# Token halves for the last three tiles of two down projections in a one-core encoder layer

## The chip, the cores and the metric

One core of a Trainium2 chip runs the whole program. Its engines are TensorE (PE in the views; PEld is its weight load), VectorE (DVE), ScalarE (ACT), GpSimd (POOL) and SyncE (SP), which issues most DMAs. The metric is the device time in microseconds, the median of several runs.

## What is computed

The reference, cut to the layer (DEPTH is 1, 512 tokens of width 1024, 16 meta tokens in front, so 528 rows until the last of them are dropped):

```python
h = layer_norm(concatenate([meta, x]), ln_in_g, ln_in_b)
h = layer_norm(ALPHA * h + 0.5 * swiglu(h, gate1, up1, down1), ffn1_ln_g, ffn1_ln_b)
h = layer_norm(ALPHA * h + token_mixer(h, ...), mix_ln_g, mix_ln_b)
h = layer_norm(ALPHA * h + 0.5 * swiglu(h, gate2, up2, down2), ffn2_ln_g, ffn2_ln_b)
return h[:, 16:]
# swiglu: (silu(h @ gate) * (h @ up)) @ down, inner width 2816
# token_mixer: h @ w_in, then windowed attention and a two-way gated linear attention, then @ w_out
```

## The kernel before

Activations lie transposed: eight tiles of 128 features (KD = 8), each with all tokens in its free dimension. Every float32 product is made of three fp16 products: weights and activations are split into a high and a low half, and `PRODUCTS` lists the three pairs.

**Weights.** A chunk of weights is loaded into one of two buffers of `stage`. VectorE takes the largest value of each partition (`chunk_max`, L1413), GpSimd takes the largest over the partitions, VectorE works out a power of two in four small operations (`chunk_scale`, L1395 to L1400), ScalarE writes the high half (`split_hi`, L1059) into one of two buffers of `wsp`, and VectorE the low half (`chunk_lo`, L1435), which raises `w_ready`. Each engine's order is written out by hand. SyncE loads chunk c once chunk c - 2 is split.

**Down projection of either feed-forward block (`ffn`, f = 0 or 1).** Eight tiles q = 0 to 7 of the output, each of 22 slices of the inner width. The last three slices have a scale of their own and sum into other banks, so VectorE adds a tile in two steps, A (L1471, against `H`) and B (L1459, against `X`), and then adds the tile into `x_sum` (L1356). In the first block a tile is 132 matmuls of 264 columns, in the second 66 of 512. Chunks 0 and 1 of the down weights are split before the projection starts. In step q VectorE prepares the chunk of tile q + 1 (for q of 1 to 6) and then adds tile q. TensorE may start tile q when its weights are ready and tile q - 2 has been added.

**Norm (`layer_norm(L)`).** L = 1 and 3 follow the two feed-forward blocks, L = 2 the mixer. For each of two token halves: TensorE makes the mean by a matmul with a matrix of ones (`sum_tiles`, L499, and the last tile, L504), VectorE subtracts it (`centre`, L1363), ScalarE squares (L992), TensorE sums the squares (L510), ScalarE takes the root (L1042), VectorE the reciprocal (L1382). Then, tile by tile over all tokens, VectorE multiplies (L1386), ScalarE writes the fp16 input `xs` of the next matmuls and `H` (L1051, L1053), VectorE the low half of `xs` (L1376). After L = 3 SyncE writes `H` out.

**Start of the mixer.** `w_in` is used in 20 tiles: z (0), gk (1, 2), gq (3, 4), gv (5 to 16) and others. TensorE runs tiles 0 and 1 as the norm delivers `xs` (L632), then the others (L648), with small gate matmuls (L695) between. ScalarE empties each tile (`proj_out`, L1121), and a tile may start when the tile two before it is out. `gates_abs` (L1151) and `gates_ln` (L1158, L1160) are the start of the gate arithmetic on ScalarE; `gates` on VectorE carries it on.

Of the kernel before, what the change touches and what calls it, by code (L numbers as in the profile page):

```python
# [102 lines left out]
def build(nc, x_in, meta_in, params, rel_in, head_in, ident_in, masks_in, reset_in, w2_in,  # L103
          gate, up, down, w_in, w_out, out):
    with ExitStack() as ctx:
# [279 lines left out]
        GK, GQ, GV, GG, AQ, AK, AV = 1, 3, 5, 5 + 2 * NCH, 9 + 2 * NCH, 13 + 2 * NCH, 14 + 2 * NCH  # L385
        LAST_OF = [max(n for n, t in enumerate(TILES) if t[2] == c) for c in range(N_IN)]
# [32 lines left out]
        def ln_bank(L, square, h):  # L419
            return 4 * square + (h if L < 2 else 2 * h + 1)  # L420
# [30 lines left out]
        def _(sp):  # L451
# [15 lines left out]
            for f in range(2):  # L467
# [8 lines left out]
                with sp.Fori(0, N_DN // 2) as i:  # L476
                    for t in range(2):
                        sp.wait_ge(w_ready, DN[f] - 1 + t + 2 * i)
                        load_halves(down[f][2 * i + t], (DN[f] + t) % 2, DN_COLS)
# [14 lines left out]
        def _(pe):  # L494
            def sum_tiles(L):

                pe.wait_ge(x_summed, sums_before(L) + N_SUM)
                for h in range(2):
                    nc.tensor.matmul(PS[:, ln_bank(L, 0, h), 0:ln_width(L)], ones[:, :], x_sum[:, token_half(L, h)], start=True, stop=False)  # L499

            def layer_norm(L):
                for h in range(2):
                    pe.wait_ge(*((res_half, L) if h == 0 else (res_done, 2 + KD * L)))
                    nc.tensor.matmul(PS[:, ln_bank(L, 0, h), 0:ln_width(L)], ones[:, :], X[:, KD - 1, token_half(L, h)],  # L504
                                     start=False, stop=True).then_inc(mean_ready, 1)
                for h in range(2):
                    for k in range(KD):
                        n = ln_step(L, h, k)
                        pe.wait_ge(squared, n + 1)
                        nc.tensor.matmul(PS[:, ln_bank(L, 1, h), 0:ln_width(L)], ones[:, :], squares[:, n % 4, 0:ln_width(L)],  # L510
                                         start=k == 0, stop=k == KD - 1).then_inc(sq_added, 1)
# [62 lines left out]
            def res_tile(late, r, s, w, src, kt, k_sem=None, k0=0, norm=None, split_at=None, before_b=None):  # L574


                pe.wait_ge(res_done, r + 1)
                for k in range(kt):
                    if norm is not None and k == kt - 3:
                        sum_tiles(norm)  # L580
                    if k == split_at:
                        mm.then_inc(res_ready, 1)
                        if before_b is not None:
                            pe.wait_ge(*before_b)
                    if k_sem is not None:

                        pe.wait_ge(k_sem, k0 + k + 1)
                    b = split_at is not None and k >= split_at
# [1520 lines left out]
```

## Time and profile before

| | |
|---|---|
| Time, median of 3 runs | 1091.84 us (1091.57 to 1091.97) |
| Time of the profiled execution | 1082.67 us |
| Its span, first to last instruction | 1080.9 us |
| TensorE busy | 997.0 us (92%) |
| VectorE busy | 720.4 us (67%) |
| ScalarE busy | 382.2 us (35%) |
| Mean granted TensorE clock | 0.978 |

The span is the time between the first and the last instruction in the trace; the rest of the execution's time lies around it. Times below are microseconds from the span's start. A busy share is a mean over the whole span and says nothing of a single stage.

### The profile page before, as it was taken

What the parts mean: (1) busy time and instruction counts of PE and PEld (TensorE: products, weight loads), DVE (VectorE), ACT (ScalarE), POOL (GpSimd) and SP (SyncE); (2) the same over time, 40 slices, a digit from 0 to 9 for tenths busy, and PEclk for the clock granted to TensorE, in tenths of its full rate; (3) what the DMA queues carried; (4) which work ended last, traced back from release to release, by engine and by line L of the source; (5) the groups of instructions that cost most, each with busy time, mean ns of one, the idle gap of its engine ahead of it and who ended that gap; (6) DMA issues with size and microseconds to landing.
All of it is one profiled execution on the core that took longest, in us unless ns stands there. A gap on an engine that the chain in (4) does not pass through costs nothing.

```text
span 1080.9 us, 16392 instructions
## 1 busy us (share of the span) xinstructions
PE 997.0 (92%) x6605; PEld 654.4 (61%) x6605; DVE 720.4 (67%) x1186; ACT 382.2 (35%) x488; POOL 32.3 (3%) x96
## 2 busy tenths in 40 slices
PE   3999999999899988999996889699999999989995
PEld 2888888888688875985564434434444444434443
DVE  6766666668755667767659757666666667966645
ACT  5422222224411126754334741462222223531105
POOL 0000000000000000000000000000000000000000
PEclk9999999999899998999998999889999999999998
DMA  5323232323232121111211003112323223322202
GB/s 203 107 79 109 85 110 84 109 86 110 105 108 85 68 78 32 62 64 42 77 40 40 1 1 117 40 73 83 116 78 116 96 98 127 111 78 86 104 1 79
DMA packets 23808, 88.76 MB, mean 82 GB/s; under 512 B 2907, under 2 KB 3251, under 8 KB 23763
## 3 DMA queue, kind: packets, MB, share of 16 engines
q1 hardware_dynamic: 22752, 87.17, 22.7%
q10 hardware_dynamic: 1011, 0.99, 0.3%
q8 instruction: 29, 0.48, 0.2%
q14 instruction: 16, 0.13, 0.0%
HBM read 86.05 MB, written 2.10 MB: 82 GB/s over the span
## 4 chain that ended last, share of the span: by engine, by line
PE 75%; DVE 16%; ACT 6%; issue 2%; DMA 0%; ACTq 0%; POOL 0%; DVEq 0%
PE PS L553 35%; PE PS L593 20%; PE PS L648 8%; DVE cmax L1413 3%; DVE wsp L1435 3%; PE PS L944 3%; ACT wsp L1059 2%; PE PS L510 2%; PE PS L632 1%; DVE big L1513 1%; ACT H L1053 1%; PE PS L770 1%; DVE X L1363 1%; PE PS L922 1%; PE PS L766 1%
## 5 line engine op out<-in xcount | busy, mean ns | idle before, releaser
L553 PE MATMUL PS<-xs,wsp 128*128 128x264 f16 (+1 forms) x3168 | 472.7, 312 | 7.5 <-ACT xs L1051 4.0
L553 PEld LDWEIGHTS PS<-xs,wsp 128*128 128x128 f16 x3168 | 311.0, 98 | 168.4 <-issue 9.6
L1059 ACT ACTIVATE wsp<-stage,wscale 128x2048 f16<-128x2048 f32 (+2 forms) x73 | 156.5, 2144 | 369.9 <-DVE wscale L1399 198.0
L1435 DVE SCALAR_TENSOR_TENSOR wsp<-stage,wscale,wsp 128x2048 f16<-128x2048 f32 (+2 forms) x73 | 184.6, 2529 | 114.3 <-ACT wsp L1059 114.3
L593 PE MATMUL PS<-big,wsp 128*128 128x264 f16 (+1 forms) x1584 | 238.6, 314 | 11.6 <-DVE big L1513 9.5
L593 PEld LDWEIGHTS PS<-big,wsp 128*128 128x128 f16 x1584 | 155.8, 99 | 94.1 <-DVE big L1513 12.8
L1413 DVE TENSOR_REDUCE cmax<-stage 128x1 f32<-128x2048 f32 (+2 forms) x73 | 179.7, 2462 | 3.9
L1447 DVE SCALAR_TENSOR_TENSOR big<-PS,oscale,tmp_a 128x528 f32 (+3 forms) x44 | 33.4, 759 | 75.7 <-ACT tmp_a L1066 75.6
L1066 ACT ACTIVATE tmp_a<-PS,oscale 128x528 f32<-128x528 f32 (+1 forms) x44 | 30.5, 694 | 136.1 <-PE PS L553 136.1
L648 PE MATMUL PS<-xs,wsp 128*128 128x264 f16 (+1 forms) x384 | 67.0, 328 | 0.1
L2007 POOL PARTITION_ALL_REDUCE call<-cmax x73 | 27.9, 382 | 979.1 <-DVE cmax L1413 979.1
L648 PEld LDWEIGHTS PS<-xs,wsp 128*128 128x128 f16 x384 | 35.8, 98 | 24.4 <-issue 1.9
L944 PE MATMUL PS<-xs,wsp 128*128 128x512 f16 x192 | 42.3, 379 | 2.3 <-DVE X L1459 2.1
L648 PE MATMUL PS<-wsp,xs 128*88 128x256 f16 (+2 forms) x408 | 39.5, 257 | 1.7 <-ACT kT L1121 1.7
L1089 ACT ACTIVATE big<-big,hscale 128x528 f16<-128x528 f32 (+1 forms) x44 | 30.3, 722 | 29.1 <-DVE big L1513 26.6
L648 PEld LDWEIGHTS PS<-wsp,xs 128*88 128x88 f16 (+2 forms) x408 | 38.0, 113 | 3.5 <-ACT kT L1121 2.5
L1513 DVE SCALAR_TENSOR_TENSOR big<-big,hscale 128x528 f16<-128x528 f32 (+1 forms) x44 | 31.6, 755 | 5.0 <-ACT big L1089 3.8
L992 ACT ACTIVATE tmp_b<-X 128x256 f32<-128x256 f32 (+1 forms) x48 | 17.8, 416 | 46.6 <-DVE X L1363 45.3
L944 PEld LDWEIGHTS PS<-xs,wsp 128*128 128x128 f16 x192 | 18.5, 98 | 25.7 <-DVE wsp L1435 2.6
L510 PE MATMUL PS<-tmp_b,ones 128*128 128x256 f32 (+1 forms) x96 | 24.9, 417 | 9.9 <-ACT tmp_b L992 9.9
L1471 DVE SCALAR_TENSOR_TENSOR X<-PS,oscale,H 128x528 f32<-128x528 f32 (+1 forms) x16 | 12.2, 759 | 27.5 <-PE PS L593 27.4
L1403 DVE TENSOR_REDUCE hmax<-big (+2 forms) x44 | 30.1, 684 | 0.0
(208 smaller groups left out, 685.1 us busy)
## 6 DMA issues: line engine op xcount, KB each, us to landing
stage<-in_gate SPq DMA_DIRECT2D x44, 512.0 KB, 3.4
stage<-in_up SPq DMA_DIRECT2D x44, 512.0 KB, 4.2
stage<-in_down SPq DMA_DIRECT2D x32, 704.0 KB, 4.9
stage<-in_w_in SPq DMA_DIRECT2D x16, 512.0 KB, 4.4
stage<-in_w_out SPq DMA_DIRECT2D x8, 512.0 KB, 4.4
X<-in_x SPq DMA_DIRECT2D x4, 512.0 KB, 6.2
out_T<-H SPq DMA_DIRECT2D x8, 256.0 KB, 2.0
stage<-in_w_in SPq DMA_DIRECT2D x2, 576.0 KB, 4.4
```

The source lines that it names most:

```text
L510: nc.tensor.matmul(PS[:, ln_bank(L, 1, h), 0:ln_width(L)], ones[:, :], squares[:, n % 4, 0:ln_width(L)], start=k == 0, stop=k == KD - 1).t ...
L553: return nc.tensor.matmul(dst, w, x, start=k == 0 and wp + xp == 0, stop=k == KD - 1 and xp == 1)
L593: mm = nc.tensor.matmul(dst, w(wp, k), x, start=k in (0, split_at) and wp + xp == 0, stop=k + 1 in (kt, split_at) and xp == 1)
L648: mm = nc.tensor.matmul(dst, x if lhs_is_x else w, w if lhs_is_x else x, start=k == 0 and wp + xp == 0, stop=k == KD - 1 and xp == 1)
L944: mm = nc.tensor.matmul(acc(1, 2 * (n % 2)), w, tokens(1, xs[:, xp, k, :]), start=gla and k == REP and wp + xp == 0, stop=not gla and k == ...
L1059: nc.scalar.activation(wsp[:, slot, 0, 0:cols], stage[:, slot, 0:cols], ACT.Copy, scale=wscale[:, slot:slot + 1]).then_inc(w_hi, 1)
L1066: nc.scalar.activation(tokens(f, tmp_a[:, s, :]), acc(f, 4 * s), ACT.Silu, scale=oscale[:, slot:slot + 1]).then_inc(silu_ready, 1)
L1089: nc.scalar.activation(hid_s[:, m, 0, ln_cols(2 * f)], hid[:, m + 2, ln_cols(2 * f)], ACT.Copy, scale=hscale[:, i:i + 1]).then_inc(hs_hi, 1)
L1413: nc.vector.tensor_reduce(cmax[:, one], stage[:, slot, 0:cols], AX.X, ALU.max, apply_absolute_value=True).then_inc(w_max, 1)
L1435: nc.vector.scalar_tensor_tensor(wsp[:, slot, 1, 0:cols], stage[:, slot, 0:cols], wscale[:, one], wsp[:, slot, 0, 0:cols], ALU.mult, ALU.s ...
L1447: nc.vector.scalar_tensor_tensor(tokens(f, hid[:, m + 2, :]), acc(f, 4 * s + 2), oscale[:, slot:slot + 1], tokens(f, tmp_a[:, s, :]), ALU. ...
L1513: nc.vector.scalar_tensor_tensor(hid_s[:, m, 1, t], hid[:, m + 2, t], hscale[:, i:i + 1], hid_s[:, m, 0, t], ALU.mult, ALU.subtract).then_ ...
```

## The change

Tiles 0 to 4 of each down projection stay whole. Tiles 5, 6 and 7 are computed first for the first token half and then for the second, and the norm of the first half is done between and beside the matmuls of the second. So the weights of the three tiles must live longer: they get three buffers in `arena` (`w_extra`). The chunks are loaded and split in the order of `DN_ORDER`, and `DN_STEPS` says which of them VectorE prepares ahead of adding each whole tile. In the first block the projections z, gk and the first gq run by token halves too, and `gates(1)` stands two tiles later. A tiny square root (`warm`) stands ahead of each norm on ScalarE. In norm 2 the low half of the first gate/up chunk, the next chunk's maximum and its scale change places. The output is written in 16 halves instead of 8 tiles. No arithmetic is left out.

```diff
+N_FULL = 5
+DN_ORDER = [0, 1, 5, 2, 3, 6, 4, 7]
+DN_AT = [DN_ORDER.index(q) for q in range(N_DN)]
+DN_STEPS = [[2], [3], [4, 5], [6], [7]]
...
+        def w_down(f, q, part):
+            return wsp[:, (DN[f] + q) % 2, part, :] if q < N_FULL else w_extra[:, q - N_FULL, part, :]
...
 TensorE, ffn(f):
+                for q in range(N_FULL):
+                    down_tile(f, q)
+                down_tile(f, 5, 0)
+                down_tile(f, 6, 0)
+                down_tile(f, 7, 0, (KF - 3, lambda: sum_tiles(L, 0)))
+                down_tile(f, 5, 1, (8, lambda: mean(L, 0)))
+                square_sums(L, 0)
+                down_tile(f, 6, 1)
+                down_tile(f, 7, 1, (KF - 3, lambda: sum_tiles(L, 1)))
...
 TensorE, mixer_projections() (mean(1, 1) stands inside first_proj_tiles(0)):
-                first_proj_tiles()
-                proj_tile(GK + 1)
+                first_proj_tiles(0)
+                early_proj_tile(GK + 1, 0)
+                square_sums(1, 1)
+                early_proj_tile(GQ, 0)
+                first_proj_tiles(1)
+                early_proj_tile(GK + 1, 1)
                 gates(0)
+                early_proj_tile(GQ, 1)
+                proj_tile(GQ + 1)
                 gates(1)
-                for n in range(GQ, GV + NCH + 1):
+                for n in range(GV, GV + NCH + 1):
...
 TensorE, at the end:
-            layer_norm(3)
+            mean(3, 1)
+            square_sums(3, 1)
...
 ScalarE, ffn(f):
+                for n in itertools.chain(*DN_STEPS):
+                    q = DN_ORDER[n]
+                    c = DN[f] + n
+                    if q < N_FULL:
+                        act.wait_ge(res_ready_b, N_RES * f + q - 1)
+                    act.wait_ge(w_scale, 4 * c + 3)
+                    nc.scalar.activation(w_down(f, q, 0), stage[:, c % 2, 0:DN_COLS], ACT.Copy,
+                                         scale=wscale[:, c % 2:c % 2 + 1]).then_inc(w_hi, 1)
...
 VectorE, ffn(f):
+                for n in range(2):
+                    down_scales(n)
+                for q in range(N_FULL):
+                    for n in DN_STEPS[q]:
+                        down_chunk(n)
+                    down_residual(f, q)
+                for n, q in enumerate(range(N_FULL, N_DN)):
+                    if f == 0 and n < 2:
+                        c = IN0 + n
+                        chunk_max(c, c % 2, c // 2, KD * IN_COLS[n])
+                        split(c, c % 2, KD * IN_COLS[n], (XF_IN, XF_INQ)[n])
+                    down_residual(f, q, 0)
+                L = 2 * f + 1
+                centre(L, 0)
+                down_residual(f, 5, 1)
+                half_rstd(L, 0)
+                half_norm(L, 0, 0, 4)
+                down_residual(f, 6, 1)
+                half_norm(L, 0, 4, KD)
+                down_residual(f, 7, 1)
+                centre(L, 1)
+                half_rstd(L, 1)
+                half_norm(L, 1, 0, KD)
```

`down_chunk(n)` is `chunk_max`, `chunk_scale`, two small scales and the low half of one chunk; `down_residual` is the old A and B with the addition into `x_sum`; `half_norm` is the tile by tile part of the norm for one token half.

**VectorE at the start of the first down projection.** The rows of before begin behind the last low half of the hidden values (A, L1471, and B, L1459, add a tile; L1356 sums; L1413 starts a chunk, here that of tile 2, and L1435 ends it):

```order
L1471 SCALAR_TENSOR_TENSOR X<-PS,oscale,H 128x528
L1459 SCALAR_TENSOR_TENSOR X<-PS,oscale_b,X 128x528
L1441 TENSOR_TENSOR oscale<-winv,xinv 128x1
L1565 TENSOR_TENSOR oscale_b<-winv,xinv 128x1
L1413 TENSOR_REDUCE cmax<-stage 128x1
L1395 TENSOR_SCALAR cexp<-call 128x1
L1397 TENSOR_SCALAR cneg<-cexp 128x1
L1399 TENSOR_SCALAR wscale<-cneg 128x1
L1400 TENSOR_SCALAR winv<-cneg 128x1
L1435 SCALAR_TENSOR_TENSOR wsp<-stage,wscale,wsp 128x2816
```

The rows of the change begin behind the scales of chunks 0 and 1 (L1516 starts a chunk, L1693 ends it; L1569 and L1573 are A and B):

```order
L1516 TENSOR_REDUCE cmax<-stage 128x1
L1498 TENSOR_SCALAR cexp<-call 128x1
L1500 TENSOR_SCALAR cneg<-cexp 128x1
L1502 TENSOR_SCALAR wscale<-cneg 128x1
L1503 TENSOR_SCALAR winv<-cneg 128x1
L1682 TENSOR_TENSOR dscale<-winv,xinv 128x1
L1684 TENSOR_TENSOR dscale_b<-winv,xinv 128x1
L1693 SCALAR_TENSOR_TENSOR arena<-stage,wscale,arena 128x2816
L1569 SCALAR_TENSOR_TENSOR X<-PS,dscale,H 128x528
L1573 SCALAR_TENSOR_TENSOR X<-PS,dscale_b,X 128x528
L1516 TENSOR_REDUCE cmax<-stage 128x1
```

A whole chunk, that of tile 5, which goes to `arena`, now stands ahead of adding tile 0 and of tile 2's chunk.

**ScalarE at the start of the mixer.** Before, from the emptying of z, gk and gk (L1121) on (L1151 is `gates_abs`, L1059 a high half, the table loads belong to `gates_ln`):

```order
L1121 ACTIVATE big<-PS,oscale 32x528
L1121 ACTIVATE X<-PS,oscale 128x528 x2
L1151 ACTIVATE tmp_a<-PS,par 128x528 x2
L1059 ACTIVATE wsp<-stage,wscale 128x2048
L1158 ACT_TABLE_LOAD
L1158 ACTIVATE tmp_a<-tmp_a 128x1056
L1160 ACT_TABLE_LOAD
L1160 ACTIVATE tmp_a<-tmp_a 128x1056
L1121 ACTIVATE X<-PS,oscale 128x528 x2
L1059 ACTIVATE wsp<-stage,wscale 128x2048
L1121 ACTIVATE big<-PS,oscale 88x256
```

With the change (L1194 empties, L1224 is `gates_abs`, L1122 a high half):

```order
L1194 ACTIVATE big<-PS,oscale 32x528
L1194 ACTIVATE X<-PS,oscale 128x528 x3
L1224 ACTIVATE tmp_a<-PS,par 128x528
L1122 ACTIVATE wsp<-stage,wscale 128x2048
L1194 ACTIVATE X<-PS,oscale 128x528
L1224 ACTIVATE tmp_a<-PS,par 128x528
L1231 ACT_TABLE_LOAD
L1231 ACTIVATE tmp_a<-tmp_a 128x1056
L1233 ACT_TABLE_LOAD
L1233 ACTIVATE tmp_a<-tmp_a 128x1056
L1122 ACTIVATE wsp<-stage,wscale 128x2048
L1194 ACTIVATE big<-PS,oscale 88x256
```

The second `gates_abs` moved behind the emptying of both gq tiles, and the table loads with it; the first gv tile (88x256) is still emptied behind the high half that follows them.

**VectorE at norm 2.** Before, behind the sum of tile 6 (L1464 adds tile 7, L1435 and L1413 are the first and second gate/up chunk, L1363 centres, L1382 is the reciprocal):

```order
L1464 SCALAR_TENSOR_TENSOR X<-PS,oscale,H 128x256 x2
L1435 SCALAR_TENSOR_TENSOR wsp<-stage,wscale,wsp 128x2048
L1413 TENSOR_REDUCE cmax<-stage 128x1
L1363 TENSOR_TENSOR X<-X,PS 128x256 x16
L1395 TENSOR_SCALAR cexp<-call 128x1
```

With the change, from the same place (L1538 is the low half, L1592 adds tile 7, L1434 centres, L1516 is the maximum, L1484 the reciprocal):

```order
L1538 SCALAR_TENSOR_TENSOR wsp<-stage,wscale,wsp 128x2048
L1592 SCALAR_TENSOR_TENSOR X<-PS,oscale,H 128x256 x2
L1434 TENSOR_TENSOR X<-X,PS 128x256 x16
L1516 TENSOR_REDUCE cmax<-stage 128x1
L1484 RECIPROCAL stats<-stats 128x256 x2
L1498 TENSOR_SCALAR cexp<-call 128x1
```

The low half moved ahead of adding the last tile, the maximum behind the centring, and the small scale operations behind the reciprocals.

## Rows read from the trace of the kernel before

**Rows 1.** The page, the chain that ended last, by engine

```profile
PE 75%; DVE 16%; ACT 6%; issue 2%; DMA 0%; ACTq 0%; POOL 0%; DVEq 0%
```

**Rows 2.** Timeline of TensorE, norm 1: start, us, line, count, idle before

```profile
396.75 1.16 PE L504 MATMUL PS<-X,ones 128*128 128x264 f32 x4 [0.65 <-DVE X L1464]
...
412.79 1.04 PE L632 MATMUL PS<-xs,wsp 128*32 128x264 f16 x4 [4.10 <-ACT xs L1051]
...
428.59 5.56 PE L648 MATMUL PS<-xs,wsp 128*128 128x264 f16 x48
```

**Rows 3.** Timeline of VectorE, first down projection

```profile
289.21 0.15 DVE L1441 TENSOR_TENSOR oscale<-winv,xinv 128x1 f32<-128x1 f32 x1
...
292.18 3.08 DVE L1413 TENSOR_REDUCE cmax<-stage 128x1 f32<-128x2816 f32 x1
...
299.03 3.15 DVE L1435 SCALAR_TENSOR_TENSOR wsp<-stage,wscale,wsp 128x2816 f16<-128x2816 f32 x1 [2.71 <-ACT wsp L1059]
...
306.21 0.77 DVE L1459 SCALAR_TENSOR_TENSOR X<-PS,oscale_b,X 128x528 f32<-128x528 f32 x1 [1.23 <-PE PS L593]
...
335.91 0.77 DVE L1459 SCALAR_TENSOR_TENSOR X<-PS,oscale_b,X 128x528 f32<-128x528 f32 x1 [1.23 <-PE PS L593]
336.71 0.71 DVE L1356 TENSOR_TENSOR stats<-stats,X 128x528 f32<-128x528 f32 x1
```

**Rows 4.** Timeline of VectorE, second down projection

```profile
957.42 0.15 DVE L1441 TENSOR_TENSOR oscale<-winv,xinv 128x1 f32<-128x1 f32 x1
...
972.74 0.75 DVE L1459 SCALAR_TENSOR_TENSOR X<-PS,oscale_b,X 128x512 f32<-128x512 f32 x1 [1.16 <-PE PS L593]
...
1001.23 0.75 DVE L1459 SCALAR_TENSOR_TENSOR X<-PS,oscale_b,X 128x512 f32<-128x512 f32 x1 [1.16 <-PE PS L593]
```

**Rows 5.** Windows: PE, PEld, DVE, ACT, POOL busy us, granted clock, DMA share, GB/s

```profile
279.00:283.50 4.50, 0.00 (x0) 0.00 (x0) 3.87 (x3) 1.85 (x4) 0.00 (x0) 0.89 0.00 0
283.50:289.00 5.50, 5.48 (x26) 3.76 (x27) 4.60 (x11) 3.50 (x5) 0.00 (x0) 0.50 0.74 262
```

**Rows 6.** Timeline of ScalarE, norm 1, eight squares of one half

```profile
404.39 3.04 ACT L992 ACTIVATE tmp_b<-X 128x264 f32<-128x264 f32 x8
```

**Rows 7.** Timeline of ScalarE, start of the mixer

```profile
436.16 0.70 ACT L1151 ACTIVATE tmp_a<-PS,par 128x528 f32<-128x528 f32 x1 [0.19 <-PE PS L695]
...
440.15 1.28 ACT L1158 ACT_TABLE_LOAD   x1
...
449.68 0.47 ACT L1121 ACTIVATE big<-PS,oscale 88x256 f32<-88x256 f32 x1
```

**Rows 8.** Timeline of TensorE, start of the mixer

```profile
446.86 18.50 PE L648 MATMUL PS<-wsp,xs 128*88 128x256 f16 x168
465.30 1.15 PE L695 MATMUL PS<-big,w 32*128 32x264 f32 x4
```

**Rows 9.** Timelines of VectorE and TensorE, norm 2

```profile
681.95 2.34 DVE L1435 SCALAR_TENSOR_TENSOR wsp<-stage,wscale,wsp 128x2048 f16<-128x2048 f32 x1
...
686.41 5.38 DVE L1363 TENSOR_TENSOR X<-X,PS 128x256 f32<-128x256 f32 x16
...
700.32 1.89 DVE L1386 TENSOR_TENSOR X<-X,stats 128x512 f32<-128x512 f32 x3
...
681.70 1.13 PE L504 MATMUL PS<-X,ones 128*128 128x256 f32 x4 [0.58 <-DVE X L1464]
687.32 6.08 PE L510 MATMUL PS<-tmp_b,ones 128*128 128x256 f32 x16 [4.49 <-ACT tmp_b L992]
```

**Rows 10.** Timelines of TensorE and ScalarE, norm 3

```profile
1059.61 1.13 PE L504 MATMUL PS<-X,ones 128*128 128x256 f32 x4 [0.65 <-DVE X L1464]
...
1065.92 3.72 PE L510 MATMUL PS<-tmp_b,ones 128*128 128x256 f32 x16 [0.93 <-ACT tmp_b L992]
...
1072.70 5.75 ACT L1053 ACTIVATE H<-X,par 128x512 f32<-128x512 f32 x8 [2.55 <-DVE X L1386]
```

**Rows 11.** The page, DMA issues of the output: KB each, us to landing

```profile
out_T<-H SPq DMA_DIRECT2D x8, 256.0 KB, 2.0
```

More of the change, by code:

```diff
@@ L475, in _ @@
                         load_gu(f, 2 * i + 2 + t, (GU[f] + t) % 2)
[L476 to L479, printed above, removed]
+                for n, q in enumerate(DN_ORDER):
+                    sp.wait_ge(w_ready, DN[f] + n - 1)
+                    load_halves(down[f][q], (DN[f] + n) % 2, DN_COLS)
                 if f == 0:
@@ L493, in _, with sum_tiles @@
+            sp.wait_ge(out_done, 2 * 16 * KD)
         @block.tensor
         def _(pe):
[L495 to L499, printed above, removed]
+            def sum_tiles(L, h):
+                pe.wait_ge(x_summed, sums_before(L) + (N_SUM if L == 2 or h == 0 else KD))
+                nc.tensor.matmul(PS[:, ln_bank(L, 0, h), 0:ln_width(L)], ones[:, :], x_sum[:, token_half(L, h)], start=True, stop=False)
@@ L501, in layer_norm @@
             def layer_norm(L):
                 for h in range(2):
-                    pe.wait_ge(*((res_half, L) if h == 0 else (res_done, 2 + KD * L)))
-                    nc.tensor.matmul(PS[:, ln_bank(L, 0, h), 0:ln_width(L)], ones[:, :], X[:, KD - 1, token_half(L, h)],
-                                     start=False, stop=True).then_inc(mean_ready, 1)
+                    mean(L, h)
                 for h in range(2):
[L507 to L511, printed above, removed]
+                    square_sums(L, h)
@@ L572, in gu_tile, with down_tile @@
                 mm.then_inc(gu_ready, 1)
-            def res_tile(late, r, s, w, src, kt, k_sem=None, k0=0, norm=None, split_at=None, before_b=None):
+            def down_tile(f, q, h=None, between=None):
+                i = q if h != 1 else q + N_DN - N_FULL
+                s = i % 2
+                r = RES[2 * f + 1] + i
+                pe.wait_ge(w_ready, DN[f] + DN_AT[q] + 1)
                 pe.wait_ge(res_done, r + 1)
[L578 to L581, printed above, removed]
+                for k in range(KF):
+                    if between is not None and k == between[0]:
+                        between[1]()
+                    if k == KF_A:
@@ L582, in res_tile @@
                         mm.then_inc(res_ready, 1)
[L583 to L588, printed above, removed]
-                    for wp, xp in PRODUCTS:
-                        for h in [None] if late else range(2):
-                            dst = acc(1, 4 * b + 2 * s) if late else PS[:, 4 * b + 2 * s + h, 0:HALF]
-                            x = tokens(1, src(xp, k)) if late else src(xp, k)[:, h * HALF:(h + 1) * HALF]
-                            mm = nc.tensor.matmul(dst, w(wp, k), x, start=k in (0, split_at) and wp + xp == 0,
-                                                  stop=k + 1 in (kt, split_at) and xp == 1)
@@ L935, in out_part @@
                 if n == KD - 1 and not gla:
-                    sum_tiles(2)
+                    for h in range(2):
+                        sum_tiles(2, h)
                 for k in range(REP, KD) if gla else range(REP):
```

267 lines of the change are left out of this document (175 added, 92 removed).

## The prediction

> **What bounds the kernel now.** I read the chain of waits first: it lies on TensorE for 75% of the span and on VectorE and ScalarE for 22% [rows 1], so time can be won only where TensorE stands still, and is lost wherever a new stall stands in its way. The timelines show where it stands still. Norm 1: the last down tile ends at 396.1, z and gk end at 428.6 [rows 2], 32.5 us in which TensorE has 10.8 us of projection work (96 matmuls of 264 columns; a down tile of 132 takes 14.85 [rows 3]). Norm 2: its centring starts at 686.4 behind two chunk operations, although the mean began at 681.70 [rows 9]. Norm 3: the last tile ends at 1058.96 and the span at 1080.9, 21.9 us [rows 10]. These three places are what the change can win on.
>
> The other thing to see is how full VectorE is in the down projections. Its step for one whole tile is a chunk and an addition. A chunk is 3.08 (maximum), the small operations, 2.71 of waiting for ScalarE's high half, and 3.15 (low half): from 292.18 to 302.18, **10.0 us** [rows 3]. An addition is A, B and the sum, 0.77 + 0.77 + 0.71, **2.2 us** where nothing is waited for. That is 12.2 us of a tile of 14.85 us (306.2 to 335.9 are two tiles) or, in the second projection, 14.25 (972.7 to 1001.2) [rows 3, 4]. Its slack is 2 to 2.6 us a tile, and it is strictly in order.
>
> **The change part by part.**
>
> *Order of the chunks.* VectorE reaches the down projection at 289.2 (second: 957.4) [rows 3, 4]. Before, it added tile 0 at once and then prepared tile 2. Now it does tile 5's chunk first, adds tile 0, and only then does tile 2's. With 0.3 for four small scales and 1.5 for adding tile 0 (no sum), tile 2's weights are ready at 289.2 + 0.3 + 10.0 + 1.5 + 10.0 = 311.0. TensorE ends tile 1 at 306.2 [rows 3], so it waits 4.8. In the second projection: 957.4 + 21.8 = 979.2 against 972.7 [rows 4], a wait of 6.5. Then follow adding tile 1 (2.2), the chunks of tiles 3 and 6 (20.0), adding tile 2 (2.2) and the chunk of tile 4 (10.0): ready at 311.0 + 34.4 = 345.4 and at 1013.6. Tile 4 began at 335.9 and 1001.2 [rows 3, 4]. So VectorE, not TensorE, now sets its start: **+9.5** and **+12.4**. Queued behind these chunks are the additions, but banks and tiles that wait for them are not late. The loads aren't either: each was issued two chunks ahead. Chunk 7 is ready at 345.4 + 2.2 + 10.0, before TensorE ends tile 4, and from there the half tiles have what they need; the two chunks of the projections fit (tile 6's sum is there about 1 us before it is asked for).
>
> *From tile 4 to the last half tile.* The f16 work is the same. New ahead of the last tile's end are one mean (half of 1.13, 0.6) and eight square sums, 3.72 for 256 columns [rows 10], 3.8 for 264. In the second projection 66 matmuls of 512 columns become 132 of 256 in three tiles: 14.25/66 is 215.9 ns, 2.6 ns over 512 columns at 2.4 GHz, so each further matmul costs 2.6 ns, 0.5 in all. First: 345.4 + 60.2 (four tiles of 14.85 and 0.9 of `sum_tiles`) + 4.4 = 410.0. Second: 57.7 became 57.7 + 4.8, so **+4.8**.
>
> *Norm 1's second half and the early projections.* From 410.0 TensorE has the first halves of z and gk (5.5), the mean (0.6), the second gk (2.7), eight square sums (3.8): 422.6. The way from the last square sum to the first `xs` was 4.1 [rows 2]; with half width tiles in the multiplication and in `xs` 0.7 less: 426.0, covered to 425.3 by gq's first half. Then ScalarE delivers `xs` and `H` of a tile in 2 x 0.38 [rows 6], eight tiles in 6.1, slower than TensorE uses them (0.68): gk ends at about P = 432.5. Before, this was 428.6, with 5.5 us more of gk and gq still to do.
>
> *The gates.* Before, from P = 428.6: gv begins at 446.86, P + 18.3 [rows 8]. Now the remaining half tiles, a gq tile and two gates (2.7 + 1.0 + 2.7 + 5.4 + 1.0) end at P + 12.8, when gv could start 5.5 us nearer. But the second `gates_abs` comes only behind the second gates, and the table loads behind it. From the first table load to gv's first tile being out were 10.0 us (440.15 to 450.15) [rows 7]. Now: P + 12.9 + 0.7 + 10.0 = P + 23.6. The third gv tile waits for that, and TensorE is there at P + 12.8 + 2 x 2.64 = P + 18.1 (seven gv tiles in 18.50 [rows 8]): **a stall of 5.5**, which takes back what the halves won. The fourth gv tile's bank is freed the same 2 us later relative to P, 1.5 us more of waiting. `gates(2)`, at 465.3 before, starts at P + 38.3 = 470.8: **+5.5** for all of the first block and norm 1.
>
> *Norm 2.* The centring waits only for the mean: 682.4 instead of 686.4. TensorE then stands still too briefly for its clock to fall, so the first square sums take 3.72 and not 6.08 [rows 9, 10]; the small scale operations now stand after the reciprocals, +0.8. 700.3 becomes 695.1, **-5.2**. The moved low half lies under the last tile's matmuls; the maximum under the square sums.
>
> *Norm 3.* From the last tile's end T: B 0.5, mean 0.7, centring starts at T + 1.4; square sums end at T + 6.0; root, reciprocal and multiplication as 1069.64 to 1072.70 before, less 0.35: T + 8.8; eight `H` at 0.38, and SyncE's issue and the landing (2.4 from the last `H` to the end; 2.0 of it landing [rows 11]): T + 14.2, with 0.6 for SyncE issuing more often than every 0.4 us: T + 14.8 instead of T + 21.9, **-7.1**.
>
> *The clock.* Behind 4.7 us in which TensorE stood still, its granted clock fell and stayed at 1.2 GHz for 5.5 us [rows 5], which costs half of that time. The first stall of each down projection is followed by a second that VectorE sets, and absorbs this. Behind the gv stall, 1.5 us of waiting absorb a part; the second stall of the second projection (5.9 less what the slow clock took) may bring a fall of its own. Bounds 0 and 2 x 2.8 = 5.5; I take **+1.6**, since half of it is absorbed at the one place and the other is uncertain. The Trainium skill, TensorE: Matmul & The Clock Gate, section What's actually happening, says that the throttled state is the default and activity releases it; by that rule, too, each new stall of this length is paid twice, and the sum would stand at its upper end, 5.5.
>
> **Sum.** 5.5 - 5.2 + (12.4 + 4.8 - 7.1) + 1.6 = **+12.0 us**. The profiled execution's span was 1080.9 and its own time 1082.67, 9.2 below the median of 1091.84; a difference should carry over, so the span becomes 1092.9 and the median **1103.8**.
>
> **The rivals.** *VectorE keeps up* (faster): if tile 2's and tile 4's weights were in time, 9.5 + 12.4 would be gone and the time 1082. That needs tile 2's weights at 306.2, so 16.7 us for two chunks and an addition that take 21.8 by the rows; a chunk would have to take 7.6 us. For it speaks only that a chunk holds 2.71 of waiting on ScalarE; no row shows one below 10. Chance 0.05. *The stalls come smaller*: ScalarE's gate chain is hidden as before, or the norm delivers earlier; the gv stall and the clock vanish, -5.5 - 1.6: 1097. Against it, ScalarE's order is fixed. Chance 0.08. *Every stall cools TensorE* and no wait absorbs it, with the low clock of the half tiles on top: 4 further us, 1108; chance 0.1. *The small output pieces*: 128 KB instead of 256 KB each, 1.05 MB in the last half. If pieces could follow each other no faster than those of 256 KB did (5.75/8, 0.72 us apart [rows 10]) the end would come 8 x 0.34 = 2.7 later: 1106.5; 0.05. The Trainium skill, DMA: Bandwidth & Descriptors, section Bandwidth, calls small transfers descriptor-dominated (138 GB/s at 64 KB); by an estimate from that figure the last 1.05 MB takes 7.6 us. Nothing at all, because TensorE's waits moved but didn't grow: 0.03 for a time within 0.2%.
>
> **How the numbers follow.** The forecast has 0.69. Its own bounds are the clock (0 to 5.5, so -1.6 and +3.9) and some 2 us for the gate chain either way: 1100 to 1109. With the smaller stalls below and the costlier cases, 1097 to 1110 leaves out the faster case and what neither sum holds. Within 0.2% is about what a measurement can tell from no change. Faster 0.05 (the first rival), same 0.03, slower 0.92 (all others, 0.69 + 0.08 + 0.10 + 0.05).
>
> **What would show it.** In the profile after: TensorE waiting for VectorE's low half (L1693) about 4.8 and 6.5 us ahead of down tile 2, and 2 to 5 us ahead of tile 4; about 5 us ahead of the third gv tile, released by ScalarE (L1194); norm 2's centring within 1 us of the mean; the last down half tile near 410 and, behind norm 2, the tail at 15 us. I would be wrong if chunks ran faster than 10 us, or if TensorE stood still elsewhere: at a half tile's start for an addition that VectorE has not reached.

## The result and the profile after

The changed kernel takes **1104.2 us** (median of 4 runs, 1102.3 to 1105.7) against 1091.7 us for the kernel before in the same comparison: a ratio of 1.0125, 95% interval 1.0091 to 1.016. It is slower, as predicted (1103.8). The profiled execution of the change has a span of 1100.5 us, TensorE busy 1008.0 us and a mean granted clock of 0.969.

The two traces lie 19.6 us apart, more than the medians. The kernel before repeats less well than three runs had shown: over all comparisons its 45 timed executions (median 1090.8 us) lie in three groups, near 1083, 1086 and 1092 us, all of them below the change's lowest of 1102.3, and its profiled execution (1082.67 us) is in the lowest group. So sizes are taken below from stages of the traces, and medians only say which kernel is faster.

The page's chain of waits has less of TensorE and more of VectorE than in [rows 1]:

```profile
PE 65%; DVE 21%; ACT 9%; issue 4%; POOL 0%; DMA 0%; ACTq 0%; DVEq 0%
```

The timeline of TensorE in the down projections, the waits for a low half (L1693) in the brackets:

```profile
310.71 32.02 PE L627 MATMUL PS<-big,wsp 128*128 128x264 f16 x264 [5.45 <-DVE wsp L1693]
344.88 16.69 PE L627 MATMUL PS<-big,wsp 128*128 128x264 f16 x132 [2.14 <-DVE wsp L1693]
...
989.03 31.30 PE L624 MATMUL PS<-big,wsp 128*128 128x512 f16 x132 [5.69 <-DVE wsp L1693]
1023.09 14.42 PE L624 MATMUL PS<-big,wsp 128*128 128x512 f16 x66 [2.77 <-DVE wsp L1693]
1086.14 0.70 PE L522 MATMUL PS<-X,ones 128*128 128x256 f32 x2 [0.64 <-DVE X L1573]
```

These are tiles 2 and 3 as one row and then tile 4, once for each block; the last row is the mean behind the last half tile. In the kernel before TensorE runs through from tile 0 far into tile 7 without one wait, in the first block and in the second:

```profile
283.52 109.66 PE L593 MATMUL PS<-big,wsp 128*128 128x264 f16 x948 [4.73 <-DVE big L1513]
951.84 104.32 PE L593 MATMUL PS<-big,wsp 128*128 128x512 f16 x474 [4.77 <-DVE big L1513]
```

The timeline of TensorE at the start of the mixer, which answers to [rows 2] and [rows 8]:

```profile
410.94 1.84 PE L662 MATMUL PS<-xs,wsp 128*32 128x264 f16 x12
412.62 0.61 PE L522 MATMUL PS<-X,ones 128*128 128x264 f32 x2
413.16 5.38 PE L662 MATMUL PS<-xs,wsp 128*32 128x264 f16 x36
...
429.34 7.71 PE L662 MATMUL PS<-xs,wsp 128*32 128x264 f16 x46 [0.55 <-DVE xs L1454]
...
460.93 15.41 PE L684 MATMUL PS<-wsp,xs 128*88 128x256 f16 x120 [5.44 <-ACT big L1194]
476.27 1.15 PE L732 MATMUL PS<-big,w 32*128 32x264 f32 x4
```

The last half tile ends at 411.0 where a whole one ended at 396.1, and the third group of gate matmuls ("third gates" from here on, `gates(2)`; the next group is the fourth) starts at 476.27 where it started at 465.30. Norm 2, which answers to [rows 9]:

```profile
697.42 1.13 PE L522 MATMUL PS<-X,ones 128*128 128x256 f32 x4 [0.58 <-DVE X L1592]
699.08 3.72 PE L529 MATMUL PS<-tmp_b,ones 128*128 128x256 f32 x16 [0.53 <-ACT tmp_b L1036]
...
711.95 1.01 PE L578 MATMUL PS<-xs,wsp 128*128 128x512 f16 x2 [4.56 <-ACT xs L1096]
```

From the mean to the first matmul on the new `xs` it takes 14.53 us, and took 20.31. The 19.6 us come together as follows, with the boundaries read from TensorE's timeline. "Hidden values in" is the end of TensorE's wait for them, at 283.5 us in the kernel before and within 0.3 us of it in all. The two last columns are kernels of the experiments.

| Stage, us | before | change | e1_order | e7_natural |
|---|---|---|---|---|
| first down projection, hidden values in, to the fourth gates | 185.61 | 196.78 | 193.03 | 179.14 |
| fourth gates to norm 2's mean | 212.57 | 217.32 | 217.32 | 216.15 |
| mean to first `xs` matmul | 20.31 | 14.53 | 14.53 | 14.53 |
| to the second down projection | 249.83 | 249.83 | 249.83 | 249.83 |
| second down projection, hidden values in, to the end | 129.06 | 138.72 | 131.19 | 127.71 |

### The profile page after: what moved, and what is told of

Its sections match the earlier page's. It is cut to its first block, busy times and chain, and to the rows that moved or that the text cites. A ratio compares the mean times of both kernels' runs of the same rounds, so it can differ in the third digit from the quotient of the medians.

```text
span 1100.5 us, 16765 instructions
## 1 busy us (share of the span) xinstructions
PE 1008.0 (92%) x6803; PEld 673.6 (61%) x6803; DVE 727.0 (66%) x1224; ACT 390.3 (35%) x515; POOL 32.4 (3%) x96
## 4 chain that ended last, share of the span: by engine, by line
PE 65%; DVE 21%; ACT 9%; issue 4%; POOL 0%; DMA 0%; ACTq 0%; DVEq 0%
PE PS L578 35%; PE PS L622 8%; PE PS L684 7%; DVE cmax L1516 5%; PE PS L988 3%; DVE wsp L1538 3%; ACT wsp L1122 2%; PE PS L529 2%; DVE big L1629 2%; PE PS L627 2%; ACT wsp L1178 1%; PE PS L662 1%; PE PS L624 1%; PE PS L965 1%; DVE wsp L1693 1%
## 5 line engine op out<-in xcount | busy, mean ns | idle before, releaser
L578 PEld LDWEIGHTS PS<-xs,wsp 128*128 128x128 f16 x3168 | 310.3, 98 | 169.9 <-issue 9.4
L1122 ACT ACTIVATE wsp<-stage,wscale 128x2048 f16<-128x2048 f32 (+2 forms) x61 | 124.9, 2047 | 245.5 <-DVE wscale L1502 200.0
L1538 DVE SCALAR_TENSOR_TENSOR wsp<-stage,wscale,wsp 128x2048 f16<-128x2048 f32 (+2 forms) x61 | 146.8, 2406 | 83.1 <-ACT wsp L1122 83.1
L1516 DVE TENSOR_REDUCE cmax<-stage 128x1 f32<-128x2048 f32 (+2 forms) x73 | 179.7, 2461 | 3.9
L627 PE MATMUL PS<-big,wsp 128*128 128x264 f16 x660 | 80.9, 289 | 13.0 <-DVE wsp L1693 7.6
L624 PE MATMUL PS<-big,wsp 128*128 128x512 f16 x330 | 77.3, 398 | 14.6 <-DVE wsp L1693 8.5
L622 PE MATMUL PS<-big,arena 128*128 128x264 f16 (+1 forms) x792 | 89.4, 274 | 0.0
L622 PEld LDWEIGHTS PS<-big,arena 128*128 128x128 f16 x792 | 77.5, 98 | 11.5
L627 PEld LDWEIGHTS PS<-big,wsp 128*128 128x128 f16 x660 | 67.1, 102 | 26.9 <-DVE wsp L1693 8.2
L624 PEld LDWEIGHTS PS<-big,wsp 128*128 128x128 f16 x330 | 32.9, 102 | 59.0 <-DVE wsp L1693 9.4
L684 PEld LDWEIGHTS PS<-xs,wsp 128*128 128x128 f16 x384 | 36.2, 99 | 25.5 <-issue 4.2
L684 PE MATMUL PS<-wsp,xs 128*88 128x256 f16 (+2 forms) x408 | 41.8, 265 | 7.1 <-ACT big L1194 5.4
L1178 ACT ACTIVATE wsp<-stage,wscale 128x2816 f16<-128x2816 f32 x6 | 15.9, 2642 | 55.4 <-DVE winv L1503 55.4
```

The lines of the kernel that those rows point to most:

```text
L578: return nc.tensor.matmul(dst, w, x, start=k == 0 and wp + xp == 0, stop=k == KD - 1 and xp == 1)
L622: mm = nc.tensor.matmul(PS[:, bank, 0:ln_width(2 * f)], w, x[:, token_half(2 * f, h)], **flags)
L624: mm = nc.tensor.matmul(acc(1, bank), w, tokens(1, x), **flags)
L627: mm = nc.tensor.matmul(PS[:, bank + g, 0:HALF], w, x[:, token_half(0, g)], **flags)
L684: mm = nc.tensor.matmul(dst, x if lhs_is_x else w, w if lhs_is_x else x, start=k == 0 and wp + xp == 0, stop=k == KD - 1 and xp == 1)
L1122: nc.scalar.activation(wsp[:, slot, 0, 0:cols], stage[:, slot, 0:cols], ACT.Copy, scale=wscale[:, slot:slot + 1]).then_inc(w_hi, 1)
```

## Experiments

The questions were: does the loss stand in the order of VectorE's chunks or in the halves themselves; is the stall at gv a matter of ScalarE's order; what is the order in norm 2 worth alone; and what is left when the orders are put right. Two more kernels and four repeated profiles then asked about what the first four had left open. No kernel leaves out arithmetic.

**e1_order.** The change with chunks in the order of use:

```diff
-DN_ORDER = [0, 1, 5, 2, 3, 6, 4, 7]
+DN_ORDER = [0, 1, 2, 3, 5, 4, 6, 7]
-DN_STEPS = [[2], [3], [4, 5], [6], [7]]
+DN_STEPS = [[2], [3], [4], [5], [6, 7]]
```

> The change with the chunks split in the order of use: tiles 2, 3 and 4 first, chunk 5 after them (DN_ORDER 0 1 2 3 5 4 6 7 with one chunk a step, two in the last). My theory: the 9.5 and 12.4 us that the first and second down projection lose stand in the order of VectorE's chunks. Expected: no wait ahead of tile 2, tile 4 starting at about 336.3 and 1001.9 instead of 344.9 and 1023.1; then smaller new waits at the half tiles (1.4, 2.7 and 3 us in the first block, 2.3 in the second), since VectorE still has the same eight chunks to prepare. In all some 13 us below the change. Rival: the halves themselves cost the time (more instructions, half-wide operations), and the waits only move: then it is less than 4 us below the change.

Measured: 1091.25 us, ratio to before 1.0035 (1.0009 to 1.0061), 11.0 us below the change by the spans. TensorE's timeline, first block and then tile 4 of the second:

```profile
335.69 15.02 PE L627 MATMUL PS<-big,wsp 128*128 128x264 f16 x132 [0.46 <-DVE wsp L1693]
359.22 7.58 PE L622 MATMUL PS<-big,arena 128*128 128x264 f16 x66 [1.07 <-DVE X L1573]
369.32 8.24 PE L622 MATMUL PS<-big,arena 128*128 128x264 f16 x57 [2.52 <-DVE X L1573]
378.78 0.71 PE L514 MATMUL PS<-stats,ones 128*128 128x264 f32 x2 [1.22 <-DVE stats L1441]
...
1010.08 14.42 PE L624 MATMUL PS<-big,wsp 128*128 128x512 f16 x66 [1.56 <-DVE wsp L1693]
```

The wait ahead of tile 2 is gone and smaller ones stand at the half tiles: TensorE now waits for additions (L1573), the first behind two down chunks in a row, each of the next two behind a chunk of the projections. The 1.56 us ahead of tile 4 in the second block was not expected; its chunk stands behind tile 5's. By the spans 11 us were won where some 13 were expected, so two lists of numbers account for more than half of the 19.6. What is left here, 8.6 us, is still partly waits, and whether the halves themselves cost anything only the last kernels tell.

**e2_gv_out.** The change with ScalarE emptying two gv tiles earlier:

```diff
-                projection_hi(3)
                 proj_out(GV)
-                decays(0, 0)
                 proj_out(GV + 1)
+                projection_hi(3)
+                decays(0, 0)
```

> The change, with ScalarE emptying the first two gv tiles ahead of the high half of the weights that stood in front of them. My theory: the 5.4 us stall ahead of the third gv tile is ScalarE's order (gates, table loads, high half, then the first gv tile). But the first gv tile stays behind the table loads, so the bank comes free when they are over, at about 453 instead of 460.3: the stall shrinks from 5.4 to below 1 us and the slow clock behind it goes, 5 to 7 us below the change. Rival: the wait goes to the next tiles or to the gates, because the high half is then late for the weights behind it, and the time does not change (within 1 us).

Measured: 1102.84 us; to the fourth gates 195.22 us against 196.78. The theory got the first wait right and missed the next. TensorE's timeline at gv:

```profile
456.35 5.41 PE L684 MATMUL PS<-wsp,xs 128*88 128x256 f16 x48 [0.66 <-ACT big L1194]
465.32 9.66 PE L684 MATMUL PS<-wsp,xs 128*88 128x256 f16 x72 [3.56 <-ACT big L1194]
```

and ScalarE's in the same stretch:

```profile
455.76 0.81 ACT L1194 ACTIVATE big<-PS,oscale 88x256 f32<-88x256 f32 x2
458.62 2.00 ACT L1122 ACTIVATE wsp<-stage,wscale 128x2048 f16<-128x2048 f32 x1 [2.05 <-DVE wscale L1502]
...
464.72 0.46 ACT L1194 ACTIVATE big<-PS,oscale 88x256 f32<-88x256 f32 x1
```

Both gv tiles are out by 456.6. But the high half (L1122) waits 2.05 us for a scale that VectorE makes behind gate arithmetic, and the third gv tile is emptied (464.72) only behind that high half and five decays. Of the stall of 5.44 us 0.66 is left in its place and 3.56 came back two tiles later. The rival was right that the wait moves, not in its reason: no weights come late, the emptying does. And the gain, 1.6 us in the stage, is a little more than its 1 us.

**e3_norm2_only.** The kernel before with only the new order in norm 2 on VectorE (ahead of adding tile 7 the low half, behind the centring the maximum, behind the reciprocals the scale):

```diff
+                    if last and t:
+                        chunk_lo(c + 1, (c + 1) % 2, cols)
...
-            chunk_lo(GU[1], GU[1] % 2, GU_COLS)
-            chunk_max(GU[1] + 1, (GU[1] + 1) % 2, (GU[1] + 1) // 2, GU_COLS)
```

> The kernel before with one part of the change alone: in norm 2 the low half of the first gate/up chunk stands ahead of adding the last tile, the next chunk's maximum behind the centring and its scale behind the reciprocals. My theory: 5.2 to 5.8 us below the kernel before, with the centring within 1 us of the mean and the first square sums at 3.72 us instead of 6.08. Rival: the moved operations are only met later (the second gate/up chunk late), and the gain is under 2 us.

Measured: 1080.81 us against 1086.46 for the kernel before in that comparison, ratio 0.9947 (0.9917 to 0.9977). From the mean to the first `xs` matmul 14.59 us, so 5.7 were won there (4.3 by the spans, 1080.9 and 1076.6). TensorE's timeline, norm 1 and norm 2:

```profile
399.03 5.51 PE L510 MATMUL PS<-tmp_b,ones 128*128 128x264 f32 x16 [2.23 <-ACT tmp_b L992]
...
683.94 3.72 PE L510 MATMUL PS<-tmp_b,ones 128*128 128x256 f32 x16 [0.53 <-ACT tmp_b L992]
```

The second row is the gain: 3.72 us where [rows 9] show 6.08. The first is a warning: norm 1 is untouched here, and behind the same wait of 2.23 us the same sixteen matmuls take 5.51 us in this execution; in the first profile of the kernel before they took 3.83 (from 400.13).

**e6_reordered.** The change with the orders of e1 and e2, and VectorE's extra chunks spread out (on ScalarE the high half of the second projection chunk moves with them, into norm 1's squares):

```diff
+                    if n == 0:
+                        down_chunk(N_DN - 1)
+                    if n == 2 and f == 0:
+                        chunk_max(IN0, IN0 % 2, IN0 // 2, KD * IN_COLS[0])
+                        split(IN0, IN0 % 2, KD * IN_COLS[0], XF_IN)
                     down_residual(f, q, 0)
...
                 centre(L, 1)
+                if f == 0:
+                    c = IN0 + 1
+                    chunk_max(c, c % 2, c // 2, KD * IN_COLS[1])
+                    split(c, c % 2, KD * IN_COLS[1], XF_INQ)
```

> The change with every order that my reading blames put right: chunks in the order of use, the last down chunk and the two projection chunks spread between the half tiles' additions and behind the first half's centring, and the first gv tiles emptied ahead of the high half. No arithmetic differs. My theory: the stalls at tiles 2 and 4, at the half tiles and at gv go, and what is left are the gains at norms 1, 2 and 3: about 28 us below the change, near 1076, some 15 below the kernel before. Rival: VectorE has no room for the extra work beside the half tiles, so that the waits stand elsewhere: then it is within 5 us of the first of these four kernels.

Measured: 1081.51 us, ratio 0.9944 (0.9917 to 0.9971): 22.7 below the change, not 28, and 5 below the kernel before, not 15. No half tile waits any more. What was missing showed in TensorE's timeline: 0.46 and 1.56 us ahead of tile 4 (its chunk stood behind tile 5's), 0.67 and 3.57 at gv as in e2, and 7.7 us more than before between the fourth gates and norm 2, at a slower clock (below); the span of this profile, 1082.0, is even 1.1 us above that of the kernel before.

**e7_natural.** e6_reordered with orders meant to take those four waits away:

```diff
-DN_ORDER = [0, 1, 2, 3, 5, 4, 6, 7]
+DN_ORDER = [0, 1, 2, 3, 4, 5, 6, 7]
...
 ScalarE:
                 projection_hi(3)
-                decays(0, 0)
                 proj_out(GV + 2)
+                decays(0, 0)
+                proj_out(GV + 3)
...
 VectorE:
-                gates(0)
                 projection_scale(3)
+                gates(0)
```

> The reordered kernel of the last call (e6_reordered) with what its trace showed as waits taken away: chunks in their natural order 0 to 7, so that tile 4's weights are not behind tile 5's; the third gv tile emptied right behind the high half, and the fourth between the two groups of decays; the scale of that chunk ahead of VectorE's gate arithmetic. My theory: these waits are worth what they showed, 0.46 and 1.56 us ahead of tile 4 and 0.67 + 3.57 us at gv, so that it stands 5 to 6 us below e6_reordered in the stages (down projections and start of the mixer). Rival: VectorE's chunks have no room elsewhere either, the half tiles then wait by 1 to 3 us, and the gain is below 3 us.

Measured: 1073.87 us, ratio 0.9871 (0.9836 to 0.9906). To the fourth gates it takes 5.6 us less than e6_reordered, in the second down projection 1.2 less. ScalarE's timeline at gv:

```profile
443.79 0.81 ACT L1195 ACTIVATE big<-PS,oscale 88x256 f32<-88x256 f32 x2
444.50 2.00 ACT L1124 ACTIVATE wsp<-stage,wscale 128x2048 f16<-128x2048 f32 x1
447.21 0.47 ACT L1195 ACTIVATE big<-PS,oscale 88x256 f32<-88x256 f32 x1 [0.71 <-PE PS L684]
```

The high half follows at once, and the emptying of the third gv tile waits for TensorE, where TensorE had waited 3.57 us for it. The waits ahead of tile 4 are gone. Not all is: 0.67 us ahead of the third gv tile and 0.15 ahead of the fifth are left, and 0.88 for VectorE stands new ahead of the fourth gates. This kernel beats both: against the kernel before it wins 6.5 us up to the fourth gates, 5.8 in norm 2 and 1.4 in the second down projection, and gives 3.6 back in the attention: 10.0 by the spans (1080.9 and 1070.9).

**e8_z_first.** e7_natural with the 24 matmuls of z ahead of the 24 of gk in the first half:

```diff
-                for k, n in itertools.product(range(KD), range(2)):
+                pairs = [(k, n) for n in range(2) for k in range(KD)] if half == 0 else itertools.product(range(KD), range(2))
+                for k, n in pairs:
```

> e7_natural with the first half's z projection whole, then the first half's gk, where both alternated tile by tile before. It tests the 48 matmuls of that stage, which took 6.9 us and not the 5.4 that matmuls of 264 columns take elsewhere. Theory: changing between weights of 32 and of 128 columns costs the 0.037 us each, and z first wins about 1.4 us up to the end of this stage. Rival: the time is in the start of the stage whatever the order, and nothing changes.

Measured: 1074.95 us, ratio 0.9877 (0.9846 to 0.9908), not to be told from e7_natural; but in the stage itself the theory holds. TensorE's timeline of the 12 and 36 matmuls that took 1.84 and 5.38 us in the change:

```profile
399.60 1.52 PE L663 MATMUL PS<-xs,wsp 128*32 128x264 f16 x12
...
401.70 4.33 PE L663 MATMUL PS<-xs,wsp 128*32 128x264 f16 x36
```

and the timeline of weight loads, first of the change, which alternates,

```profile
411.38 0.23 PEld L662 LDWEIGHTS PS<-xs,wsp 128*128 128x128 f16 x3 [0.22 <-issue]
411.83 0.22 PEld L662 LDWEIGHTS PS<-xs,wsp 128*32 128x32 f16 x3 [0.22 <-issue]
```

then of e8_z_first, which changes once:

```profile
401.70 1.24 PEld L663 LDWEIGHTS PS<-xs,wsp 128*32 128x32 f16 x12 [0.34 <-issue]
403.15 2.59 PEld L663 LDWEIGHTS PS<-xs,wsp 128*128 128x128 f16 x24 [0.22 <-issue]
```

A pause of 0.22 us stands at each change between a load of 32 and one of 128 columns. From the first matmul of z to the second gk tile, with norm 1's mean between (its weights have 128 columns too), it is 6.26 us (399.60 to 405.86) instead of 7.43 in e7_natural (399.18 to 406.61): 1.17 us, where 1.4 was expected, for 3 changes of width instead of 15, 0.1 us each. The change of PSUM bank, which goes with it here, is not the cause: a whole down tile of the first block changes bank at each of its 132 matmuls, with 128 columns throughout, and takes 14.85 us, 0.1125 each, no more than the 24 matmuls of the second gk tile in one bank (2.70 us, 418.37 to 421.07 in the change).

**The kernels unchanged, profiled again.** The change once, the kernel before three times.

> The changed kernel, unchanged, profiled once more, for the same question. Theory: the stalls ahead of tile 2 (5.45 and 5.69), tile 4 (2.14 and 2.77) and gv (5.44) repeat within 0.3 us, and the stretch from the third gates to norm 2's mean (221.1 us) is what varies.

> The kernel before, unchanged, profiled once more. It asks how far two executions of one kernel differ and where. Theory: everything up to the end of the start of the mixer (465 us) and from norm 2 on (682 us) repeats within 0.5 us, and what differs between executions is TensorE's granted clock in the attention between them, by up to 9 us. Rival: the difference is spread over all stages.

> The kernel before, unchanged, profiled a third time. Its timed executions lie near 1083, 1086 and 1091.7 us, and the two profiled ones both at 1082.7 to 1082.9. Theory: an execution of 1086 or more has its extra time between 465 us (third gate matmuls) and 682 us (norm 2's mean), at a granted clock of 0.5 to 0.9 behind short waits there, since that stage took 216.4 us in both profiles and 221 to 224 in kernels whose attention is the same. Rival: the extra time is spread over all stages. If this execution is near 1083 again it tells neither.

> The same once more, for the same question and with the same expectation as the third profile of the kernel before.

Measured: 1103.55 us for the change; 1082.86, 1082.65 and 1085.68 for the kernel before. Two of the latter repeat the first profile. The third is 3.0 us longer, all of it between the gates and norm 2: the windows of that stretch in the profile shown before, and 20 us of it,

```profile
465.30:681.70 216.40, 196.60 (x1285) 116.03 (x1285) 148.37 (x363) 95.16 (x178) 3.69 (x10) 0.98 0.13 45
610.00:630.00 20.00, 18.02 (x108) 8.65 (x104) 13.58 (x61) 13.87 (x37) 0.00 (x0) 0.91 0.00 0
```

and in b4_before_fourth:

```profile
465.16:684.56 219.40, 199.87 (x1286) 116.99 (x1285) 148.46 (x363) 95.15 (x178) 3.69 (x10) 0.96 0.13 44
610.00:630.00 20.00, 18.02 (x102) 8.87 (x100) 12.87 (x58) 12.99 (x34) 0.00 (x0) 0.84 0.00 1
```

The same work at a granted clock (third number from the end) of 0.96 instead of 0.98: TensorE is busy 3.3 us longer. In the change's second profile the waits are 5.04 and 5.76 us ahead of tile 2, 1.74 and 2.84 ahead of tile 4, and 5.44 at gv; two of them differ by 0.4 from the first, more than expected, and this time tile 4 of the first block ran at full clock (1.00) behind its wait. So not the attention alone varies, as was expected: up to the fourth gates it took 194.67 us instead of 196.78, and from there to norm 2's mean 220.42 instead of 217.32.

## Why the prediction was right, and where it was not

**Order of the chunks: right.** Tile 2 was to start at 311.0 and did at 310.71; tile 4 at 345.4, and did at 344.88. In the second block, counted from 951.84 and 961.78, where the hidden values are in: 27.4 us to tile 2 predicted, 27.3 measured; 61.8 to tile 4, and 61.3. e1_order takes this order away and with it 11 of the change's 19.6 us.

**From tile 4 to the last half tile: right in the second block, 1 us short in the first.** There the step took 62.4 us (62.5 predicted). In the first it ended at 411.0, not 410.0, since tile 4 took 16.69 us instead of 14.85; in the second profile, where tile 4 was not slowed, the last half tile ended at 409.6. The windows of the change, at the start of tile 2, of tile 4, behind the gv stall, and at tile 4 of the second block:

```profile
310.70:314.00 3.30, 3.29 (x16) 2.26 (x17) 3.23 (x4) 0.00 (x0) 0.00 (x0) 0.50 0.71 213
344.90:348.00 3.10, 3.10 (x19) 2.33 (x20) 3.03 (x4) 0.00 (x0) 0.00 (x0) 0.66 0.67 223
461.00:464.00 3.00, 3.00 (x15) 2.77 (x16) 2.97 (x6) 2.83 (x5) 0.00 (x0) 0.50 0.00 0
1023.10:1026.00 2.90, 2.90 (x14) 1.37 (x15) 2.83 (x4) 0.00 (x0) 0.00 (x0) 1.00 0.02 6
```

**The clock: the mechanism right, the size 0.9 short in this execution.** Behind the waits of 5.4 us the granted clock is 0.50, the lower level of 1.2 GHz. At tile 2 it costs 2.3 us (32.02 for two tiles of 14.85), and tile 4's wait absorbs that, as predicted. But tile 4's own wait of 2.14 us brought a fall that nothing absorbs (1.8), and so did the gv stall (15.41 us for five tiles of 2.64: 2.2). That makes 4.0, but the sum already held 1.5 us of waiting for the fourth gv tile's bank, and in the trace the slow clock fills just that time, so 2.5 came on top where +1.6 was taken. The wait of 2.77 us in the second block brought none, and neither did the one of 1.74 in the second profile. The Trainium skill, TensorE: Matmul & The Clock Gate, What's actually happening, calls the throttled state the default that activity releases. The trace agrees behind the stalls of 5 us and more; behind the shorter ones either clock was seen.

**Norm 1 and the early projections: the term of the sum that was mis-sized.** "Then ScalarE delivers `xs` and `H` of a tile in 2 x 0.38" took the rate of the squares [rows 6] for an operation of another kind. ScalarE's timeline of the change:

```profile
427.65 0.61 ACT L1114 ACTIVATE xs<-X,par_s 128x264 f16<-128x264 f32 x1 [2.34 <-DVE X L1460]
428.17 0.59 ACT L1116 ACTIVATE H<-X,par 128x264 f32<-128x264 f32 x1
428.67 0.59 ACT L1114 ACTIVATE xs<-X,par_s 128x264 f16<-128x264 f32 x1
429.16 0.59 ACT L1116 ACTIVATE H<-X,par 128x264 f32<-128x264 f32 x1
```

They follow each other every 0.50 us, 1.0 a tile, so from the first `xs` matmul (428.40) to P = 437.05 it was 8.65 us instead of 6.5: +2.1. Before, at 528 columns, the pace was 0.72; halving the columns saves 0.22 of it, and the rest is paid twice as often. The Trainium skill, ScalarE: Activation LUTs, What ACT_TABLE_LOAD costs, gives 186 ns and 0.833 ns a column, 93 ns more for each per-partition scale or bias, and 93 ns of overlap in a row. An estimate from these figures is 0.59 us alone and 0.50 in a row at 264 columns with both operands, and the trace agrees: 0.59, and 0.50 apart. It would have given the term beforehand. A further 1.4 us went where z and gk alternate (6.9 us for 48 matmuls, without the mean between them; 5.5 predicted); e8_z_first shows why.

**The gates: right in kind.** The stall ahead of the third gv tile was to be 5.5 us and is 5.44. ScalarE's timeline of the change, as predicted: table loads, then a high half, then the first gv tile.

```profile
453.27 1.28 ACT L1233 ACT_TABLE_LOAD   x1
454.57 1.08 ACT L1233 ACTIVATE tmp_a<-tmp_a 128x1056 f32<-128x1056 f32 x1
458.42 2.00 ACT L1122 ACTIVATE wsp<-stage,wscale 128x2048 f16<-128x2048 f32 x1 [2.78 <-DVE wscale L1502]
460.33 0.45 ACT L1194 ACTIVATE big<-PS,oscale 88x256 f32<-88x256 f32 x1
```

But I read it as ScalarE's order, and the 2.78 us in the third row are VectorE's. e2_gv_out moved ScalarE's order alone and won 1.6 us; e7_natural moved both and left 0.8 of waits at gv. No run moved VectorE's alone. For the whole step +5.5 was predicted and +11.0 measured (465.30 to 476.27): 1.0 at tile 4, 1.4 for alternating, 2.1 for ScalarE's rate, 0.9 behind the gv stall.

**Norm 2: right.** -5.2 predicted, -5.8 measured, and -5.7 with this part alone (e3_norm2_only).

**Norm 3: right.** The tail behind the last tile was to be 14.8 us and is 15.0 (from 1085.5), the second block +10.1 and is +9.7. The eight `H` took 0.50 each, not 0.38, and the 0.6 that had been added for issuing smaller output pieces did not come on top: from the last `H` to the end it is 2.1 us (1098.4 to 1100.5), and a piece lands in 1.7. The rival of the small pieces did not come: no 0.72 us a piece shows, and the whole last half was out 5.6 us after its first `H`, where 7.6 was the estimate. ScalarE's timeline and the page's line of the output, which answer to [rows 10] and [rows 11]:

```profile
1094.32 4.04 ACT L1116 ACTIVATE H<-X,par 128x256 f32<-128x256 f32 x8 [2.28 <-DVE X L1460]
```

```profile
out_T<-H SPq DMA_DIRECT2D x16, 128.0 KB, 1.7
```

**The sum, and what carried it to the median.** +12.0 us was predicted and the traces show +19.6: 5.5 short in the first block, 4.8 in the attention, which the sum put at nothing without a word, while norm 2 and norm 3 gave 1.0 more than predicted and the 1.6 for the clock are part of these stages. The forecast of the median, 12.0 above 1091.84, was met because a second step failed the other way: "a difference should carry over" from the profiled execution to the median. The kernel before was profiled in its lowest group, some 9 us below the median then known; the change was profiled at its own lowest, 1.9 below its median. The clocks of the timed executions say what kind of error this is: in the kernel before the mean granted clock was 0.978 to 0.98 near 1083 us, 0.975 near 1086 and 0.970 to 0.972 near 1092, in all 41 whose clock was taken, so its groups differ by the clock; the change had 0.967 to 0.970 in all four. The prediction set the difference of two traces on a median with a slower clock than its trace had. The match of 1103.8 with 1104.2 is luck, two errors of some 7 us that cancel. That the kernel is slower, and by which waits, does not hang on it.

**What stays open.** The stretch from the gates to norm 2 took 212.6 or 215.6 us, from the fourth gates on, in profiles of the kernel before, and 216.2 to 220.4 in all kernels with halves, whose code there is the same but for the low half that VectorE does earlier at norm 2, and e3_norm2_only, which has that too, took 212.6. The windows, of the kernel before and of the change:

```profile
469.13:681.70 212.57, 192.78 (x1257) 112.81 (x1257) 147.01 (x357) 93.32 (x176) 3.69 (x10) 0.98 0.14 45
480.10:697.42 217.32, 197.62 (x1258) 113.65 (x1257) 149.45 (x358) 94.85 (x178) 3.71 (x10) 0.95 0.14 46
```

TensorE is busy 4.8 us longer on the same matmuls, at 0.95 instead of 0.98, and that is the whole 4.8 us: the loss there is the clock, as in b4_before_fourth. In the kernels with halves it was 0.94 to 0.96 in every profile. Why it is lower there, whether by when the halves let the attention begin or by something else, no run tells apart. Nor was an execution of the kernel before near 1092 us caught in a profile.

## What to carry to other kernels

An engine that prepares weights in strict order has a slack per tile (here 2 to 2.6 us); what is moved ahead of a chunk that is due sooner is paid by TensorE as soon as it is longer than that, so order such work by when it is needed, and spread what is extra one piece a step. Splitting an operation in half does not halve it: take the rate of the same kind of instruction, with its pointer operands, at the half width. And before calling a stall one engine's order, look whether the instruction in front of it is itself waiting.

## What the runs showed of the hardware that was not expected

- Changing between weight loads of 32 and of 128 columns costs TensorE 0.1 us each time (1.17 us over 12 changes), with a pause of 0.22 us between the loads.
- The same wait does not always bring the same clock: behind 2.23 us ahead of the square sums of norm 1, sixteen matmuls took 3.83 us in one execution and 5.51 in another; behind 1.74 us tile 4 kept 1.00, behind 2.14 the mean over its first 3 us was 0.66, and behind 2.77 it kept 1.00.
- One kernel's timed executions fell into three groups 3 and 6 us apart, each with a mean granted clock of its own (0.978 to 0.98, 0.975, 0.970 to 0.972), and four profiled executions all into the two upper clocks.
